# Two of the four weight-block sums of every slot made by GpSimd, the other two by VectorE from them

## The reference

```python
x = x + 0.5 * swiglu(rms_norm(x, ffn1_norm[l]), ffn1_w_gu[l], ffn1_w_down[l])
x = x + hybrid_mixer(...)
x = x + memory_cross_attention(...)
x = x + 0.5 * swiglu(rms_norm(x, ffn2_norm[l]), ffn2_w_gu[l], ffn2_w_down[l])

def swiglu(h, w_gu, w_down):
    g, u = jnp.split(h @ w_gu, 2, axis=-1)
    return (silu(g) * u) @ w_down
```

## Time and profile before

| | |
|---|---|
| median of 3 runs | 2381.81 us (2378.78 to 2386.38) |
| the profiled execution's own time | 2384.12 us |
| its span | 2382.3 us |
| granted TensorE clock, mean | 0.984 |
| weights read from HBM | 336.47 MB, 142 GB/s over the span |
| the four feed-forward blocks of the first model | from about 25, 605, 817 and 1381 us on |

### The profile page before, as it was taken

The page is one execution under the profiler, slowest core; times in us unless marked ns, Lnnn a source line. Parts: engine busy times, 40 slices in busy tenths (PEclk is TensorE's granted clock), DMA queues, the critical chain, the costliest instruction groups (busy, mean ns, idle before and its releaser), DMA issues.

```text
span 2382.3 us, 35601 instructions
## 1 busy us (share of the span) xinstructions
PE 2306.2 (97%) x14595; PEld 2098.1 (88%) x14595; DVE 1234.9 (52%) x2596; ACT 370.6 (16%) x847; POOL 112.5 (5%) x203
## 2 busy tenths in 40 slices
PE   7998999999999999999999999999999999999998
PEld 7998898788999999989878899998788888878887
DVE  5775325633666666532463467654745503556531
ACT  1210212301121022021230112102300001310000
POOL 1110000000111011000000011100000000000000
PEclk9998999999999999999999999998999999899999
DMA  7654642334564565565243456555345546426542
GB/s 215 173 160 137 150 144 98 114 119 129 161 176 160 160 170 159 180 147 152 89 123 109 140 160 168 162 152 131 96 121 154 149 156 136 122 71 175 152 151 83
DMA packets 522282, 339.83 MB, mean 143 GB/s; under 512 B 44508, under 2 KB 510216, under 8 KB 522120
## 3 DMA queue, kind: packets, MB, share of 16 engines
q1 hardware_dynamic: 517520, 334.49, 48.6%
q10 hardware_dynamic: 4328, 2.02, 0.3%
q0 software_dynamic: 272, 1.05, 0.1%
HBM read 336.47 MB, written 1.05 MB: 142 GB/s over the span
## 4 chain that ended last, share of the span: by engine, by line
PE 75%; issue 11%; DVE 9%; DVEq 2%; ACTq 1%; ACT 1%; DMA 0%; POOLq 0%; POOL 0%
PE bank L578 25%; PE bank L797 20%; PE bank L831 9%; PE bank L634 9%; PE bank L587 4%; DVE arena L1516 2%; DVE work L1516 1%; PE bank L978 1%; ACTq L1229 1%; PE bank L973 1%; PE bank L1092 1%; DVE arena L1519 1%; DVE hT L1516 1%; DVE topw L1974 0%; DVE small L1992 0%
## 5 line engine op out<-in xcount | busy, mean ns | idle before, releaser
L578 PE MATMUL bank<-hT,ring 128*128 128x256 f32 x3264 | 716.6, 382 | 6.9 <-DVE work L1519 4.1
L578 PEld LDWEIGHTS bank<-hT,ring 128*128 128x128 f32 x3264 | 622.5, 191 | 95.3 <-issue 10.1
L797 PE MATMUL bank<-work,arena 128*128 128x128 f32 x1824 | 229.6, 275 | 3.0 <-ACT topw L1316 3.0
L797 PEld LDWEIGHTS bank<-work,arena 128*128 128x128 f32 x1824 | 216.2, 192 | 3.8 <-ACT topw L1316 3.8
L634 PE MATMUL bank<-work,ring 128*128 128x256 f32 x960 | 210.8, 381 | 0.0
L634 PEld LDWEIGHTS bank<-work,ring 128*128 128x128 f32 x960 | 181.0, 190 | 29.3 <-issue 5.3
L1516 DVE TENSOR_TENSOR arena<-ring 128x512 f32<-128x512 f32 (+1 forms) x248 | 172.1, 734 | 46.7 <-PE bank L831 43.2
L578 PE MATMUL bank<-xg,ring 128*128 128x256 f32 x768 | 174.1, 384 | 0.5 <-DVE xg L1512 0.4
L578 PEld LDWEIGHTS bank<-xg,ring 128*128 128x128 f32 x768 | 144.9, 192 | 21.1 <-DVE xg L1512 1.5
L797 PE MATMUL bank<-hT,ring 128*128 128x128 f32 x1216 | 160.6, 275 | 0.0
L1519 DVE SCALAR_TENSOR_TENSOR xT<-bank,xT 128x256 f32<-128x256 f32 (+1 forms) x80 | 40.5, 528 | 222.4 <-PE bank L634 221.1
(11 more groups left out here) (293 smaller groups left out, 2599.6 us busy)
## 6 DMA issues: line engine op xcount, KB each, us to landing
ring<-in_ffn_w_gu SPq DMA_DIRECT2D x176, 512.0 KB, 5.0
ring<-in_ffn_w_up SPq DMA_DIRECT2D x84, 512.0 KB, 5.1
ring<-in_ffn_w_down SPq DMA_DIRECT2D x82, 512.0 KB, 4.4
ring<-in_w_in SPq DMA_DIRECT2D x78, 512.0 KB, 5.0
ring<-in_w_in SPq DMA_DIRECT2D x26, 1024.0 KB, 4.9
ring<-in_ffn_w_down SPq DMA_DIRECT2D x20, 1024.0 KB, 4.8
ring<-in_w_out SPq DMA_DIRECT2D x16, 1024.0 KB, 4.9
ring<-in_ca_w_kv SPq DMA_DIRECT2D x8, 1024.0 KB, 5.1
```

What stands on the lines that cost most here:

```text
L578: mm = pe.matmul(b[0:width, 0:S], view[:, c, a:a + width], src[:, c, :], start=(k == 0), stop=(k == C - 1))
L797: mm = pe.matmul(out_, a[:, c, :], b_[:, c, :], start=(start and c == 0), stop=(c == 3), skip_group_check=True)
```

## The change

GpSimd makes s1 and s3 of every slot, VectorE waits for them (`sums_begun`) and makes s2 and s4. GpSimd's program gets an order of its own in each block: the sums of slots 0 to 2 are begun first (behind the norm's `power`), then `turned_sums(0)`, then for j = 1 to 9 `turned_sums(j)` and two slots (2j + 1 and 2j + 2), then `turned_sums(10)` and the last ten slots. Before it begins a slot, GpSimd waits, as VectorE did and still does, for the slot's load and for the buffer.

```diff
+            begun = [0]
+            def begin_sums(count):
+                for _ in range(count):
+                    i = begun[0]
+                    begun[0] += 1
+                    loaded, _, (r, js) = sum_slots[i]
+                    if i >= 3:
+                        pool.wait_ge(sem[sum_slots[i - 3][1][0]], sum_slots[i - 3][1][1])
+                    pool.wait_ge(sem[loaded[0]], loaded[1])
+                    a11, a12, a21, a22 = blocks_up(r) if js is None else blocks_down(r, js)
+                    s1, s2, s3, s4 = sums_of(i, P, 4) if js is None else sums_of(i, S, js)
+                    pool.tensor_tensor(s1, a21, a22, ALU.add)
+                    pool.tensor_tensor(s3, a11, a21, ALU.subtract).then_inc(sem["sums_begun"], 1)
+
+            def ffn_s(memory_too=False):
+                begin_sums(3)
+                for j in range(N_J):
+                    if j == 4 and memory_too:
+                        power(mem_rstd[:, :], mem_ms[:, :], 2, "mem_rstd_done")
+                    turned_sums((j,))
+                    if 0 < j < N_J - 1:
+                        begin_sums(2)
+                begin_sums(2 * len(PASS) - 2)
+
             for l in range(DEPTH):
                 power(rstd[:, :], ms[:, :], 2)
-                turned_sums(range(4))
-                if l == 0:
-                    power(mem_rstd[:, :], mem_ms[:, :], 2, "mem_rstd_done")
-                turned_sums(range(4, N_J))
+                ffn_s(l == 0)
                 for _ in range(3):
                     power(rstd[:, :], ms[:, :], 2)
-                turned_sums(range(N_J))
+                ffn_s()
...
                 s1, s2, s3, s4 = sums_of(i, P, 4) if js is None else sums_of(i, S, js)
-                tt(s1, a21, a22, ALU.add)
-                tt(s3, a11, a21, ALU.subtract)
-                v.drain()
+                v.wait_ge(sem["sums_begun"], i + 1)
                 tt(s2, s1, a11, ALU.subtract)
                 v.drain()
                 tt(s4, a12, s2, ALU.subtract).then_inc(sem["sums_made"], 1)
```

More of the change, by code:

```diff
@@ L287, in build @@
                "rstd_spread",
-               "sums_made", "product_done", "snapped", "t_ready", "tg_ready", "turn_done", "turn_kept",
+               "sums_made", "sums_begun", "product_done", "snapped", "t_ready", "tg_ready", "turn_done", "turn_kept",
                "halves_turned", "turned_used", "keys_turned", "keys_doubled",
```

## The result

The changed kernel takes 2437.84 us (median of 4 runs, 2433.65 to 2438.34) against 2380.52 us for the kernel before: a ratio of 1.0232, 95% interval 1.0211 to 1.0254, 57 us slower. The profiled execution took 2438.34 us, its span is 2436.5 us, its granted clock 0.984 as before.

The account below looks back on a forecast made before the run. TensorE, busy 97%, was taken to bound the kernel. Steps 35 - 1, second matmuls +2.4, the long wait -4.8 and heads 0 gave +31.6 us on 2381.81: 2413 us, own range 2398 to 2432, 8 in 10 2374 to 2450.

Parts of the forecast that it names:

- the stall at even f: First matmuls, line 797: TensorE waits for VectorE's row at even f, 1.1 us in 32 places, 35 us in all.
- second matmuls: Line 831, after the steps: +2.4 us for late slot 21 and -4.8 us around the sines and slot 28.
- One GpSimd addition of 512 columns: GpSimd's sums s1 and s3: each lasts 1.24 us, starts 1.20 apart and holds the shared part for 1.04 us.
- both bounds: Limits for GpSimd's 512-column addition: 0.78 us by the memset slope, 1.84 us if all of 0.46 is in proportion.
- The chain of the pair: Steps, j = 2: GpSimd's sums from 63.49, row ready at 72.43, TensorE starts at 72.5 and not 71.44: 1.1 us lost.
- Pair j = 9 and slot 21: Pair j = 9 just passes with a half-size slot; slot 21 in the second matmuls costs 0.8 us, three times.
- The heads: Start of each block, slots 0 to 2: VectorE's saving against GpSimd's hold-ups, taken as 0, kept at -3 to +4 us.
- The 10.8 us wait: Line 831, slot 28: sines some 3.4 us earlier and two operations instead of four (-1.4), together -4.8 us.
- A: Rival: no blocking for the whole instruction, so no stall in the steps; 2374 to 2380 us, say 2376; chance 0.27.
- B: Rival: GpSimd's time in proportion to columns, 1.84 us an addition; 2477 us, 2460 with low hold, half way 2444; chance 0.13.
- C: Rival: VectorE spends the saved 1.4 us per slot waiting for GpSimd, so nothing moves; 2382 us; chance 0.08.

## Why the prediction was right, and where its size was off

The forecast was 2413 us, slower by the stall at even f; measured were 2438 us. Direction and mechanism held, the size did not: +57 us for +32. That is above the forecast's own range (2398 to 2432) and inside the range of 8 in 10 (2374 to 2450). No error hid another: steps, heads and second matmuls all came out slower than foreseen, by 10.5, 5.5 and 9.3 us.

*One GpSimd addition of 512 columns.* Foreseen 1.24 us, 1.20 apart; measured 1.27 and 1.22 to 1.23 (68.50, 69.73, 70.95). With 0.46 for 128 columns that is 0.19 us fixed and 2.1 ns a column. Splitting the 0.46 by what a disturbed instruction had lost was right; both bounds, 0.78 and 1.84, were far off. The Trainium skill ("GPSIMD Engine Reference", section "3.1 Elementwise — side-by-side cycle accounting") has 4497 ns for 2048 columns; a line from the 0.46 us at 128 columns here to that figure gives an estimated 1.27 us for 512. The trace agrees with its 1.27.

*The chain of the pair.* From GpSimd's first operand sum to the end of the row I had 63.49 to 72.43, 8.94 us; measured 66.47 to 75.55, 9.08. From there to TensorE's start 0.1 foreseen, 0.15 measured. With a first group of matmuls that is 0.07 longer this makes 1.35 us for 1.1: **a term mis-sized by a fifth**. The waits come at the even f and in 32 places, as foreseen. All 32 pairs together took 41.6 us where 34 had been foreseen; four of them, where TensorE has its own extra work, lost 0.5 to 0.9 us each. The other 2.9 us of the steps are in f = 3: behind a head's wait of over 2 us the first groups of matmuls ran slower in blocks 2 and 4 (below), and in blocks 1 and 3 the third product waited 1.42 and 1.53 us for ScalarE, not 0.75.

*Pair j = 9 and slot 21.* j = 9 passes without a wait, as said. Slot 21 cost 0.9 to 1.2 us in each block, 0.8 foreseen for three of them.

*The heads.* **"I take 0, and keep -3 to +4" was wrong: +5.5.** GpSimd's work on slots 0 and 1 falls beside VectorE's own additions for h and the t sums: two additions over 1024 columns that took 2.35 us took 3.42 in block 2, the next pair 3.27 for 1.29. TensorE began f = 3 0.8 to 2.4 us late in three of the four blocks. What VectorE saves at a head is less than what it is held up.

*The 10.8 us wait.* **The step that failed outright: "the sines start some 3.4 us earlier"; they started 6 us later.** I had counted VectorE's saved 1.4 us per slot and left out that the rope angles between the slots would be held as well. From the timeline of the changed kernel, between slots 22 and 23:

```profile
188.31 2.34 DVE L1542 SCALAR_TENSOR_TENSOR arena<-arena 128x256 f32<-128x256 f32 x3
188.97 1.40 POOL L1502 TENSOR_TENSOR arena<-ring 128x512 f32<-128x512 f32 x1 [4.25 <-PE bank L831]
...
190.32 1.46 POOL L1503 TENSOR_TENSOR arena<-ring 128x512 f32<-128x512 f32 x1
...
190.72 1.20 DVE L1535 TENSOR_SCALAR arena<-arena 128x256 f32<-128x256 f32 x1
```

2.34 us for three instructions that took 1.43 before, 1.20 for one that took 0.29. Together with the late slot 21, on which the first part of the angles waits, that eats the saving twice. So this item was +3.0 in block 1, with its slot 21 in it, and not -4.8. The wait of 10.8 us was to fall to about 6. It did fall, to 7.72, but TensorE had by then lost 4.2 us in three waits that were not there before (0.94, 0.87 and 2.43).

*The rivals.* A (no blocking) is refuted by the 1.65 and 1.60 us of s2 and s4, and by the kernel with the load alone. B named a size near what was measured, but for a reason that is not there: the addition is 1.27 and not 1.84 us. C is refuted by the waits at line 797. By the Trainium skill ("SBUF — State Buffer", section "Who interferes with whom") a VectorE instruction with two SBUF inputs and a GpSimd one that reads SBUF exclude each other for a whole instruction. The traces agree: a VectorE instruction of 128 columns with two SBUF inputs is held 1.07 us (1.35 for 0.28) beside a GpSimd addition of 512.

## What to carry to other kernels

Work moved from VectorE to GpSimd is only partly taken off VectorE if both read SBUF: a GpSimd addition of 512 columns costs the VectorE instruction that meets it about 1 us, short or long, if that one's inputs lie in SBUF, and the place where that falls must have slack. Where it has slack, moving work is free, but worth nothing either (2380.26 us). Order the helper's queue by when each result is wanted and by which of its inputs comes last; one swap of two calls gave back 44 of 57 us. And before relieving the engine that a wait names, follow what that engine had been waiting for: here the one large wait belonged to another queue, and moving its small loads was worth 12.7 us.

## What had not been expected

TensorE's granted clock fell behind some of the longer waits and behind none of the short ones. In the changed kernel, behind the wait of 2.06 us at the head of block 2 that ended at 636.98 (columns: stretch, its length, PE busy and instructions, granted clock, DMA share, GB/s):

```profile
630.00:635.00 5.00, 4.92 (x23) 1.00 0.63 175
636.90:639.00 2.10, 2.02 (x10) 0.56 1.14 329
639.00:641.50 2.50, 2.50 (x18) 0.69 0.36 86
641.50:645.00 3.50, 3.50 (x34) 1.00 0.02 5
```

The first group there took 1.90 us for 1.06. In the kernel before, behind the wait of 10.8 us, it was

```profile
221.70:224.00 2.30, 2.29 (x10) 0.50 0.00 0
224.00:227.00 3.00, 3.00 (x17) 0.50 0.00 0
227.00:230.00 3.00, 3.00 (x25) 0.89 0.00 0
```

0.50 is the level of 1.2 GHz, 1.00 that of 2.4 GHz. None of the 1.1 us waits in the steps shows it: from the second group on they stand 0.89 us apart again. Length alone does not decide it. In the kernel that keeps GpSimd off until the row is finished, waits of 2.10 and 2.22 us at heads left the clock at 1.00. Of its four waits for slot 21, those of 2.02 and 2.39 us brought it to 0.50 and the two of 2.04 did not. Where the clock falls, the wait costs more than its length. Moving the small loads gave 12.7 us for a wait of 10.8, and the second matmuls of block 1 became 13.9 us shorter. The slow stretches above account for the difference: 5.3 us at 0.50 and 3.0 at 0.89 lose an estimated 3 us against full clock.

VectorE's instructions with a single tensor input in SBUF were held too: `tensor_scalar` over 256 columns took 1.20 and 1.36 us beside GpSimd's additions, for 0.29 and 0.34 alone. Instructions with one of their two inputs in PSUM (`bank`) were not. From the second matmuls of the changed kernel:

```profile
212.82 1.42 DVE L1542 SCALAR_TENSOR_TENSOR xT<-e,xT 128x256 f32<-128x256 f32 x1
...
213.92 1.45 POOL L1503 TENSOR_TENSOR arena<-ring 128x512 f32<-128x512 f32 x1
...
214.17 0.41 DVE L1539 TENSOR_TENSOR e<-e,bank 128x256 f32<-128x256 f32 x1
```

`xT<-e,xT`, both inputs in SBUF, takes 1.42 us for 0.42; `e<-e,bank` takes its usual 0.41 beside GpSimd's addition. In the kernel that keeps GpSimd off until the row is finished, GpSimd's addition is not lengthened either:

```profile
121.43 1.28 POOL L1502 TENSOR_TENSOR arena<-ring 128x512 f32<-128x512 f32 x1 [2.77 <-DVE work L1541]
...
121.87 0.47 DVE L1541 TENSOR_TENSOR a<-topw,bank 128x128 f32<-128x128 f32 x2
```

So it matters not only when the moved work runs, but also which VectorE instructions it meets.

The load without the dependence cost more (93 us) than the change with it (57). Two differences bear on it, and no run separates them: VectorE still has all four sums to make, and in the changed kernel it stands still while GpSimd makes the odd slot, so that in a pair two of GpSimd's four additions meet nobody.
